# One decoder layer in f32 on one core: TensorE multiplies ones with ones in four of its waits

## The reference, cut to what matters

```python
z = rmsnorm(x, g_pre_mix) @ w_in                    # 2048 -> 5120
u, va, q, k, vb = split(z)
a_out = chunk_gmlp(gelu(u), rmsnorm(gelu(va)))      # 8 heads
b_out = rmsnorm(attend(q, k, vb, lam)) * (1 - lam_init)   # 8 heads, paged cache for the new tokens
h = x + rmsnorm(concat(a_out, b_out) @ w_out, g_post_mix)
up = rmsnorm(h, g_pre_ffn) @ w_up                   # 2048 -> 2 x 5632
c = causal_dwconv(up); gate, val = split(c)
y = h + rmsnorm((gelu(gate) * val) @ w_down, g_post_ffn)
```

## Time and profile before

| | |
|---|---|
| median of 3 runs | 2656.63 us (2655.58 to 2656.7) |
| the profiled execution | 2656.24 us |
| its span | 2654.6 us |
| granted TensorE clock, mean over the span | 0.985 |
| TensorE busy (matmul) | 2545.4 us, 96% |
| VectorE busy | 1417.1 us, 53% |
| ScalarE busy | 977.8 us, 37% |
| GpSimd busy | 644.4 us, 24% |

### The profile page before, as it was taken

How to read it: one execution, slowest core, us unless ns; L and a number is a source line. 1 busy time by engine, 2 the same in 40 slices (tenths; PEclk the granted TensorE clock), 3 DMA queues, 4 the chain that set the end, 5 groups by cost and what they waited for, 6 DMA issues and landing times.

```text
span 2654.6 us, 49458 instructions
## 1 busy us (share of the span) xinstructions
PE 2545.4 (96%) x19608; PEld 2427.1 (91%) x19608; DVE 1417.1 (53%) x2019; ACT 977.8 (37%) x1412; POOL 644.4 (24%) x515
## 2 busy tenths in 40 slices
PE   7999999999999999799999999999999999999995
PEld 7999967767778998799999999999999999999994
DVE  5000144545444468788888888888888212121115
ACT  5121133444435454444444444444444222221121
POOL 3333322112225500011111111111111433333331
PEclk9999999999999999899999999999999999999997
DMA  5333589999997563133333333333334332424221
GB/s 177 105 106 121 156 311 341 358 363 360 366 349 243 183 200 117 66 112 106 106 109 108 110 109 109 106 108 109 109 109 169 126 123 80 159 86 152 80 80 72
DMA packets 140278, 428.82 MB, mean 162 GB/s; under 512 B 16784, under 2 KB 35216, under 8 KB 138448
## 3 DMA queue, kind: packets, MB, share of 16 engines
q1 hardware_dynamic: 128128, 413.85, 46.1%
q10 hardware_dynamic: 10416, 7.92, 0.9%
q0 software_dynamic: 1568, 4.72, 0.4%
HBM read 389.83 MB, written 36.33 MB: 161 GB/s over the span
## 4 chain that ended last, share of the span: by engine, by line
PE 86%; DVE 5%; DMA 4%; SPq 2%; issue 2%; ACT 1%; POOL 0%; DVEq 0%; ACTq 0%; POOLq 0%
PE pb L2122 12%; PE pb L2124 12%; PE pb L2123 12%; PE pb L2148 7%; PE pb L2151 7%; PE pb L2150 7%; PE pb L412 5%; PE pb L414 5%; PE pb L413 5%; PE pb L2036 3%; PE pb L2038 3%; PE pb L2037 3%; PE pb L1918 2%; DMA pg<-in_kpages 2%; PE pb L1854 1%
## 5 line engine op out<-in xcount | busy, mean ns | idle before, releaser
L2122 PE MATMUL pb<-reg,uh 128*128 128x288 f32 x2408 | 716.0, 297 | 18.8 <-DVE reg L1527 8.9
L2124 PE MATMUL pb<-reg,ul 128*128 128x288 f32 x2408 | 714.7, 297 | 0.0
L2123 PE MATMUL pb<-reg,uh 128*128 128x288 f32 x2408 | 711.1, 295 | 0.0
L1000 ACT ACTIVATE uh<-ua 128x1024 fp32r<-128x1024 f32 x301 | 317.9, 1057 | 441.7 <-PE pb L2124 206.1
L2122 PEld LDWEIGHTS pb<-reg,uh 128*128 128x128 f32 x2408 | 455.5, 189 | 20.0 <-issue 12.8
L2123 PEld LDWEIGHTS pb<-reg,uh 128*128 128x128 f32 x2408 | 458.2, 190 | 0.0
L2124 PEld LDWEIGHTS pb<-reg,ul 128*128 128x128 f32 x2408 | 456.4, 190 | 0.0
L1588 DVE TENSOR_TENSOR ul<-ua,uh 128x1024 fp32r<-128x1024 f32 x301 | 367.3, 1220 | 115.0 <-ACT uh L1000 115.0
L412 PE MATMUL pb<-xh,wh 128*128 128x288 f32 x1280 | 387.1, 302 | 19.0 <-DVE xl L1242 17.3
L413 PE MATMUL pb<-xl,wh 128*128 128x288 f32 x1280 | 379.6, 297 | 0.0
L414 PE MATMUL pb<-xh,wl 128*128 128x288 f32 x1280 | 378.6, 296 | 0.0
(11 more groups left out here) (251 smaller groups left out, 4309.0 us busy)
## 6 DMA issues: line engine op xcount, KB each, us to landing
ua<-in_wstream SPq DMA_DIRECT2D x260, 512.0 KB, 3.8
pg<-in_kpages SPq DMA_DIRECT2D x128, 512.0 KB, 5.7
pg<-in_vpages SPq DMA_DIRECT2D x128, 512.0 KB, 6.1
wraw<-in_wstream SPq DMA_DIRECT2D x114, 512.0 KB, 3.7
wmore<-in_wstream SPq DMA_DIRECT2D x30, 512.0 KB, 3.7
g_d<-gv SPq DMA_DIRECT2D x44, 288.0 KB, 2.1
xh<-g_d SPq DMA_DIRECT2D x8, 1152.0 KB, 9.7
xres<-in_xT SPq DMA_DIRECT2D x4, 1152.0 KB, 6.8
```

Source lines behind the costliest of these rows:

```text
L1000: sc.activation(uh[q % SLOTS][:], ua[src][:], ACT.Copy).then_inc(u_hi, 1)
L2122: te.matmul(out, whk, xhk, start=opens and k == 0, stop=False, skip_group_check=again)
L2123: te.matmul(out, whk, xlk, start=False, stop=False, skip_group_check=again)
L2124: m = te.matmul(out, wlk, xhk, start=False, stop=k == HK - 1, skip_group_check=again)
```

## The change

A function `idle_products(bank_, n)` issues n matmuls of `ones` (128 x 128, F32R) with itself into the first 128 columns of a PSUM bank, each one a group of its own, with no semaphore. It is called in four places of TensorE's program: 60 times into bank 7 once `ones` and `ident` are there; 50 times into bank 0 after the waits behind the last head; 40 times into bank 7 between the first four `first_op` and the last four; 60 times into bank 7 ahead of the product S3 of n = 1. In the third place a wait for `sq_root` 5, which also stays where it was, is put ahead of the products: bank 7 holds `h_sums` until ACT has read it.

```diff
         pe.wait_ge(ready, 2)
+        def idle_products(bank_, n):
+            for _ in range(n):
+                te.matmul(pb[:, bank_, 0:P], ones[:].bitcast(F32R), ones[:].bitcast(F32R), start=True, stop=True)
+        idle_products(7, 60)
         def sum_squares(bank, *parts):
...
         pe.wait_ge(s["u_evac"], DB)
         pe.wait_ge(s["a_done"], DB)
+        idle_products(0, 50)
         def half_sums(bank_, *parts):
...
         h_sums(4, KD)
         first_op(A22, 0)
         pe.wait_ge(m_copied, 2 * KD)
+        pe.wait_ge(sq_root, 5)
+        idle_products(7, 40)
         for role in (A11, A21, A12, A22):
             first_op(role, 1)
         pe.wait_ge(sq_root, 5)
...
         for n in range(1, KF):
             for o in ops_of(n):
+                if n == 1 and o == O_S3:
+                    idle_products(7, 60)
                 up_op(n, o)
```

## The result

| | before | after |
|---|---|---|
| median | 2655.55 us (22 runs, 2653.09 to 2657.86) | 2659.99 us (22 runs, 2657.66 to 2662.49) |
| ratio, 95% interval | | 1.0018 (1.0011 to 1.0024) |
| span of the profiled execution | 2654.6 us | 2657.8 us |
| granted clock, mean | 0.985 | 0.986 |

The change costs 4.4 us, 0.18%. By the bound of 0.2% that the prediction named, it is no change; but over 22 runs of each it is clear of the spread, on the slower side, and 2659.99 stands inside the range while the direction was forecast wrong (-1.6).

What follows compares the result with a forecast made beforehand. The prediction took TensorE's own speed to bound the kernel. Its terms, 0 + 1.3 - 2.5 + 0 - 0.4, sum to -1.6 us, giving 2655.0 us on the median of 2656.63; range 2652 to 2660 us.

Steps and rivals of the forecast that it cites:

- place 2: Behind the last head: 50 products start at the low clock and delay the first output tile, which DVE paces; +1.3 us.
- signs of being wrong: Products spaced 0.16 us or more, place 3 running at clock 0.50, or n = 2 starting later than before.
- The price of a product: Each added 128-column product, anywhere: 0.115 us at full clock, 0.22 at the low one; floor 0.059, ceiling 0.222.
- The first rival: All places: a product costs 0.222 us at full clock, 0.44 at the low one; +8.2 us, 2664.8; chance 0.14.
- Place 1: The start: 60 products end between 11 and 15 us, lateness absorbed by TensorE's later waits for DVE; 0.
- The second rival: Products of ones neither lift nor hold the clock; place 2 costs +6.8 us, place 3 +0.2; 2663.6 us; chance 0.06.
- place 3: Between the halves of the first pair: 40 products keep the clock up for the matmuls behind them; -2.5 us.
- Place 4: Ahead of S3 of n = 1: 60 products, S3 0.8 us late but at full clock, longer wait behind; 0.
- Past the chain: ACT and DVE chain behind place 3: 2.4 of the 2.5 us gain can pass down to n = 2 at 1110.33.
- The third rival: Behind place 3, the gain does not get past the chain, only 0.7 of 2.5 us arrives; +0.4, 2657.0; chance 0.20.
- Behind it: Low-clock stretch of 5.6 us after n = 2 starts at 1110.33 falls anew when shifted; -0.4 us.
- The fourth rival: Every low stretch goes, n = 2's too, and place 2 costs nothing; -5.2 us, 2651.4; chance 0.06.

Runs made afterwards that it cites:

- the kernel that holds with 128 columns: Third place's 40 products plus 58 products of 128 columns ahead of A11 of n = 2, against the kernel before: 2654.19 us against 2655.33, ratio 0.9997.

## Why the prediction was wrong

The step that failed is place 2, and in it one sentence: "If it rises after 3.6 us (...), 16 are done by 812.65 and 34 x 0.115 = 3.9 end at 816.6". It took the delays of the 288-column matmuls for those of the products, and under these the clock did not rise at all in 10.7 us. Of the signs of being wrong that it had named, n = 2 started later than before (1114.14 against 1110.33), and the products of places 1 and 2 were over 0.16 us apart (0.214), since their clock stayed low.

- **The price of a product: right.** 0.115 and 0.22 forecast, 0.111 and 0.214 measured. The first rival (0.222 at full clock) fell. The page "TensorE: Matmul & The Clock Gate" of the Trainium skill, section "Back-to-back issue gap", has 81 ns for 128 columns; this case's 111 ns do not agree, and the one-column row beat it, as said.
- **Place 1, 0: right**, for the reason given: time within 0.4 us, and DVE's reciprocal no later. That the clock might come up under the products did not happen here either (12.9 us at 0.214); the products fitted even at the low price.
- **Place 2, +1.3 forecast, +5.3 measured** (244.15 less 238.83). 50 x 0.214 = 10.7 us bring the first real matmul to 819.9 instead of 816.6 to 817.6, and it is still at the low clock: three k steps at 0.72 and 13 at 0.40 end at 827.2, against 821.9. The second rival had the place (+6.8) and the clock that isn't raised, but the wrong reason (products of ones do not count) and a longer climb behind them (5 us; it was 2.4). Its other half, that they would not hold a clock that is up, fell in place 3. The rival got 0.06, for lack of a reason in the form of the matmul; the reason was in the rows that I had used for the price. An instruction that costs 0.122 with one moving column has its time from the weights, so this product is other work than the 288-column matmuls whose delays I borrowed. I used that row for the cost and not for the clock.
- **Place 3, -2.5: right.** -2.67 in the pair of traces; -2.0 against the mean of the nine kernels without it (19.65). The moved wait cost nothing, no DVE bound, no idle.
- **Place 4, 0: right**, and the first wait behind it grew, as forecast.
- **Past the chain: right.** A11's copy to the store is 36.3 to 36.6 us everywhere. The third rival fell.
- **Behind it, -0.4: wrong.** A low stretch at n = 2 costs nothing, for the fourth product starts when DVE's operand is there, 14.56 us behind ACT's split, at either clock. The fourth rival's 2.5 for n = 2 was not to be had either. I had priced a low clock by the matmuls in it and not by who is late next.

The time that the clock takes to fall, 3.6 to 3.8 us in the prediction, is that of one trace: it fell 2.2 us after TensorE stopped in the kernel that holds with 128 columns (1103.98 to 1106.2) and 5.0 us after in the one with place 2 alone (805.3 to 810.3, with products in the last 0.9).

The sum with the measured terms is 5.3 - 2.7 = +2.6 for the pair of profiles, and n = 2's load, 1.0 us longer in this execution, with -0.4 of smaller scatter makes it the 3.2 between the spans; for the medians 5.3 - 2.0 = 3.3 against 4.4, inside the interval (2.9 to 6.4).

The page "TensorE: Matmul & The Clock Gate" of the Trainium skill (Part 1, "What's actually happening") says that the throttle is the default and activity releases it. Here 10.7 us without a gap between instructions, PE and PEld both busy in every window shown, did not release it; if the page's rule holds here, "busy" in the profile is not the activity that it means.

## What to carry to other kernels

Products that keep TensorE warm must be put where the clock is still up, or have the form of the real work (here 288 columns, or narrow weights); 128 x 128 F32R products hold a clock but don't restore one, and cost twice as much when it is down. Before warming a stretch, look who is late next: of the five slow stretches looked at here one was worth 2 us, and four lay in front of operands that another engine was still making. And put no more products into a wait than it has room for at the low clock (here 2.1 us, nine of them).

## What the runs showed that I had not expected

- 128-column products with 128 x 128 F32R weights hold the full clock (4.4 us at 1.00 in the third place, 6.6 us ahead of n = 2) and do not raise it from 0.50 in 10.7 us, nor at the start in 12.9; the same with 32-column weights raised it after 3.4 us, 288-column ones after 3.0 us, each in one trace.
- A faster TensorE can lose its clock to its feeder: with DVE's low parts 0.68 us apart, matmuls at full clock worked 0.40 of each and fell to 0.50, where those of the kernel before, at 0.72 per k, had kept busy and rose.
- The up projection takes 930.86 to 930.89 us in 14 traces, while three other stages of the same kernels scatter by 1.3 to 3.2 us.
